# Attention scores from rounded halves: a four-layer transformer kernel on one core

## The reference, cut to what matters

```python
# even, heads 0-7: q, k normed and turned (rope); 8 query heads, 2 key heads; window of 2 chunks and a sink
scores = einsum('bcqhgd,bclhd->bchgql', qc, kb) / sqrt(64)
# even, heads 8-15: q, k normed, own keys per head, relative bias
scores = einsum('bcqhd,bclhd->bhcql', qc, kb) / sqrt(64) + bias
# odd, 8 heads, each with two query and two key parts of 64
s1, s2 = einsum(q1, k1) * scale, einsum(q2, k2) * scale; a = softmax(s1) - lam * softmax(s2)
# MLA, 8 heads: 128 plain dimensions, 64 turned ones whose key is shared by all heads
scores = (einsum(qn, k_nope) + einsum(qr, k_rope)) * scale
```

## Time and profile before

| | us |
|---|---|
| median of 3 runs (2354.4 to 2359.03) | 2355.05 |
| the profiled execution | 2356.17 |
| its span | 2354.4 |
| PE busy | 2172.7 (92%) |
| DVE busy | 1017.2 (43%) |
| ACT busy | 930.6 (40%) |
| POOL busy | 794.7 (34%) |

### The profile page before, as it was taken

How to read it: one execution, slowest core, us unless ns; L and a number is a source line. 1 busy time by engine, 2 the same in 40 slices (tenths; PEclk the granted TensorE clock), 3 DMA queues, 4 the chain that set the end, 5 groups by cost and what they waited for, 6 DMA issues and landing times.

```text
span 2354.4 us, 24410 instructions
## 1 busy us (share of the span) xinstructions
PE 2172.7 (92%) x9534; PEld 1663.5 (71%) x9534; DVE 1017.2 (43%) x1986; ACT 930.6 (40%) x1610; POOL 794.7 (34%) x367
## 2 busy tenths in 40 slices
PE   6999988988987899999979798999979996999997
PEld 5856666855554788888857587888856675888875
DVE  1145443035555246667662644430234446343214
ACT  4234333234444244555441534442244424444323
POOL 3421113432220333333214344444442224444443
PEclk9979999989888899999989899999999998999998
DMA  4210102311100221221112132233311121323331
GB/s 169 91 35 28 36 18 82 106 54 36 36 27 18 79 82 59 68 72 63 63 36 89 46 103 90 90 96 99 95 51 35 51 63 56 98 97 99 96 95 60
DMA packets 47634, 162.99 MB, mean 69 GB/s; under 512 B 5408, under 2 KB 8096, under 8 KB 47392
## 3 DMA queue, kind: packets, MB, share of 16 engines
q1 hardware_dynamic: 47088, 160.06, 21.3%
q10 hardware_dynamic: 432, 1.39, 0.2%
HBM read 159.33 MB, written 2.10 MB: 69 GB/s over the span
## 4 chain that ended last, share of the span: by engine, by line
PE 82%; DVE 10%; ACT 6%; issue 1%; DMA 0%; POOL 0%; ACTq 0%; DVEq 0%
PE ps L1451 22%; PE ps L1454 21%; PE ps L1452 21%; PE ps L1489 4%; PE ps L1505 2%; PE ps L1472 2%; DVE small L1876 1%; PE ps L1582 1%; PE ps L1497 1%; PE ps L1572 1%; PE ps L1466 1%; PE ps L1465 1%; PE ps L1463 1%; PE ps L1477 1%; DVE res L2086 1%
## 5 line engine op out<-in xcount | busy, mean ns | idle before, releaser
L2142 POOL TENSOR_TENSOR wl<-st,wh 128x1024 fp32r<-128x1024 f32 (+2 forms) x312 | 723.6, 2322 | 1372.4 <-ACT wh L1604 1372.3
L1451 PE MATMUL ps<-xh,wh 128*128 128x512 f32 x1520 | 637.0, 419 | 48.4 <-DVE xl L2090 27.9
L1454 PE MATMUL ps<-xh,wl 128*128 128x512 f32 x1520 | 602.5, 396 | 3.0 <-POOL wl L2142 3.0
L1452 PE MATMUL ps<-xl,wh 128*128 128x512 f32 x1520 | 601.6, 396 | 0.0
L1604 ACT ACTIVATE wh<-st 128x1024 fp32r<-128x1024 f32 (+2 forms) x312 | 311.4, 1003 | 240.3 <-PE ps L1454 194.1
L1451 PEld LDWEIGHTS ps<-xh,wh 128*128 128x128 f32 x1520 | 291.3, 192 | 154.5 <-issue 42.2
L1454 PEld LDWEIGHTS ps<-xh,wl 128*128 128x128 f32 x1520 | 290.7, 191 | 67.3 <-POOL wl L2142 3.8
L1452 PEld LDWEIGHTS ps<-xl,wh 128*128 128x128 f32 x1520 | 291.8, 192 | 60.7 <-issue 7.8
L2112 DVE SCALAR_TENSOR_TENSOR tmp<-ps,vec,tmp 128x511 f32<-128x511 f32 (+1 forms) x176 | 131.9, 749 | 258.1 <-ACT tmp L1781 255.0
L1451 PE MATMUL ps<-fa_h,wh 128*128 128x512 f32 x352 | 139.8, 397 | 0.0
L1454 PE MATMUL ps<-fa_h,wl 128*128 128x512 f32 x352 | 139.0, 395 | 0.0
(11 more groups left out here) (246 smaller groups left out, 3022.1 us busy)
## 6 DMA issues: line engine op xcount, KB each, us to landing
st<-in_f_up SPq DMA_DIRECT2D x88, 512.0 KB, 3.5
st<-in_s_xbc SPq DMA_DIRECT2D x32, 512.0 KB, 3.4
st<-in_f_dn SPq DMA_DIRECT2D x32, 512.0 KB, 3.5
st<-in_o_fm SPq DMA_DIRECT2D x24, 512.0 KB, 3.4
st<-in_e_fm SPq DMA_DIRECT2D x22, 512.0 KB, 3.5
st<-in_s_z SPq DMA_DIRECT2D x16, 512.0 KB, 3.5
st<-in_s_out SPq DMA_DIRECT2D x16, 512.0 KB, 3.7
st<-in_f_dn SPq DMA_DIRECT2D x16, 384.0 KB, 3.1
```

The source lines that it names most:

```text
L1451: e.matmul(u.bank.ap, hi, x.h[:, kk, :], start=first, stop=False)
L1452: e.matmul(u.bank.ap, hi, x.l[:, kk, :], start=False, stop=False)
L1454: e.matmul(u.bank.ap, lo, x.h[:, kk, :], start=False, stop=last).then_inc(S["mm"], 1)
L2142: e.tensor_tensor(P.mem["wl"][w.m % NWR][:, 0:w.n], P.mem["stage"][w.m % NSTAGE][:, 0:w.n], P.mem["wh"][w.m % NWR][:, 0:w.n].bitcast(F32), ...
```

## The change

Each query and key is split once into a rounded half and a remainder (`halves`: `head_hi` on ACT, `head_lo` on DVE). Queries of the even and odd layers go into four 128-partition tiles: hi and lo for each of the two heads, where the other head's 64 partitions are zero. The keys stay together, hi and lo. A score is then three one-pass products on 128 partitions. In MLA the plain part has three products; for the turned part one tile holds the hi of the query in one half of the partitions and its lo in the other, so that two products (by the shared key's hi and lo) suffice, five in all. MLA keys get a ring of two in the place of all eight heads. The sliding heads of the even layer are paired anew: unit j holds head j of the first group and head j of the second, so one key unit with both key heads serves all four, and the host reorders the columns of the weights. Tiles move in SBUF: the gates `sg` share the place of `yh`, and MLA's probabilities that of `xh` and `xl`.

```diff
@@ -331,7 +331,26 @@
-    def qk_prep_g(self, u, gcol, dst, rope, done=None):
+    def halves(self, src, ready, dst, parts, freed=()):
+        ends = []
+        his = [self.put("head_hi", src[rows, :], hi, ready, [dst.freed, list(freed)]) for rows, hi, lo in parts]
+        for a, (rows, hi, lo) in zip(his, parts):
+            ends.append(self.put("head_lo", src[rows, :], hi, lo, a))
+        dst.ready = ends
+        return ends
+    def split_q(self, src, ready, dst):
+        h0, h1, l0, l1 = dst.ap
+        up, down = slice(0, 64), slice(64, 128)
+        return self.halves(src, ready, dst, [(up, h0[up, :], l0[up, :]), (down, h1[down, :], l1[down, :])])
+    def split_k(self, src, ready, dst):
+        hi, lo = dst.ap
+        return self.halves(src, ready, dst, [(slice(0, 128), hi, lo)])
+    def qk_prep_g(self, u, gcol, dst, rope, key, done):
@@ -341,16 +360,17 @@
         st.release(ta)
-        g = self.tmp.take() if rope else dst
+        g = self.tmp.take()
         b = self.put("qk_n", g, u, gcol, r, tr)
...
             yield 1
-            self.rope(g, dst)
-        if done:
-            done()
+            x, g = g, self.tmp.take()
+            self.rope(x, g)
+        g.release(*(self.split_q if key == "q" else self.split_k)(g.ap, g.ready, dst))
+        done()
 
@@ -625,6 +645,8 @@
+    for h0, h1, l0, l1 in mem["qz"]:
+        P.zeroed = [P.put("zero", z) for z in (h0[64:128, :], h1[0:64, :], l0[64:128, :], l1[0:64, :])]
@@ -663,8 +685,7 @@
-    kd = [Use(Slot(mem["e_kd"][j])) for j in range(2)]
-    qs, ks = ring(mem["qs"]), ring(mem["ks"])
+    qs, ks = ring(mem["qz"]), ring(mem["kz"])
@@ -674,17 +695,16 @@
-                dst = pool if key == "k" and rope else pool.take()
+                dst = pool.take()
...
-                return P.qk_prep_g(u, P.V(gain), dst, rope, done)
+                return P.qk_prep_g(u, P.V(gain), dst, rope, key, done)
...
-        items = [item(0, 12, "a_kn", kd[0], True, "k"), item(2, 13, "a_kn", kd[1], True, "k")]
-        items[1] = (lambda: True, *items[1][1:])
+        items = [item(0, 12, "a_kn", ks, True, "k")]
...
-            items += [item(fb, 10 + fb, "b_qn", qs, False, "q"), item(fb, 14 + fb, "b_kn", ks, False, "k")]
+            items += [item(fb, 9 + fb, "b_qn", qs, False, "q"), item(fb, 13 + fb, "b_kn", ks, False, "k")]
@@ -711,22 +731,23 @@
-            kb = 2 * (fb // 2) if fb < 4 else fb
+            kb = 0 if fb < 4 else fb
...
+            kh, kl = k.ap
...
-                    h = 2 * fb + hh
-                    ro = slice(64 * hh, 64 * hh + 64)
+                    h = fb + 4 * hh if fb < 4 else 2 * fb + hh
+                    qh, ql = q.ap[hh], q.ap[2 + hh]
...
-                        v, tv = (lambda kb, g=fb // 2: va[:, kb, g * 64:g * 64 + 64]), tva
+                        v, tv = (lambda kb, g=hh: va[:, kb, g * 64:g * 64 + 64]), tva
@@ -735,11 +756,13 @@
-                    tile = Tile([(q.ap[ro, :], k.ap[ro, :])], i, kb0, n, 0.125, mx=mx.ap[:, j:j + 1],
+                    tile = Tile([(qh, kh), (ql, kh), (qh, kl)], i, kb0, n, 0.125, mx=mx.ap[:, j:j + 1],
...
-                    score(P, tile, masks, add, [q.ready, k.ready, tb])
-                    q.release(tile.scored)
-                    k.release(tile.scored)
+                    score(P, tile, masks, add, [q.ready, k.ready, tb, P.zeroed])
+                    if j == 7:
+                        q.release(tile.scored)
+                    if j == 7 and fb > 2:
+                        k.release(tile.scored)
@@ -867,14 +890,15 @@
+            kh, kl = k.ap
...
-                    ro = slice(64 * a, 64 * a + 64)
-                    tile = Tile([(q.ap[ro, :], k.ap[ro, :])], i, 0, n, 0.125, mx=small.ap[:, 4 * a + 1:4 * a + 2],
+                    qh, ql = q.ap[a], q.ap[2 + a]
+                    tile = Tile([(qh, kh), (ql, kh), (qh, kl)], i, 0, n, 0.125, mx=small.ap[:, 4 * a + 1:4 * a + 2],
@@ -882,8 +906,9 @@
-                q.release(tile.scored)
-                k.release(tile.scored)
+                if i == 3:
+                    q.release(tile.scored)
+                    k.release(tile.scored)
@@ -1275,8 +1299,10 @@
-    P.rope(g, kr)
-    qn, qr, rs, pr = (ring(mem[n], over) for n in ("m_qn", "m_qr", "r8", "m_p"))
+    krope = P.tmp.take()
+    P.rope(g, krope)
+    krope.release(*P.split_k(krope.ap, krope.ready, kr))
+    qn, kn, qr, rs, pr = (ring(mem[n], [over, x_read]) for n in ("m_qn", "m_kn", "m_qr", "r8", "m_p"))
@@ -1285,20 +1311,22 @@
-                    tk[h] = P.put("kn_in", kn[:, h, :], u, over)
-                    u.bank.release(tk[h])
+                    tk[h] = kn.take()
+                    u.bank.release(*P.split_k(u.bank.ap, u.done, tk[h]))
...
-                    q = qn.take()
-                    q.ready = [P.put("q_in", q, u)]
-                    u.bank.release(q.ready[0])
-                    got[h] = q
+                    got[h] = qn.take()
+                    u.bank.release(*P.split_k(u.bank.ap, u.done, got[h]))
...
+                    turned = P.tmp.take()
+                    P.rope(g, turned)
...
-                    P.rope(g, r)
+                    up, down = slice(0, 64), slice(64, 128)
+                    turned.release(*P.halves(turned.ap, turned.ready, r, [(up, r.ap[0][up, :], r.ap[0][down, :]),
+                                                                          (down, r.ap[1][down, :], r.ap[1][up, :])]))
@@ -1330,16 +1358,19 @@
-            q, r = got[h], rot[h // 2]
+            q, k, r = got[h], tk[h], rot[h // 2]
...
-            ro = slice(64 * (h % 2), 64 * (h % 2) + 64)
+            (qh, ql), (kh, kl), qrot, (krh, krl) = q.ap, k.ap, r.ap[h % 2], kr.ap
...
-                tile = Tile([(q.ap, kn[:, h, :]), (r.ap[ro, :], kr.ap[ro, :])], i, 0, n, scale,
+                tile = Tile([(qh, kh), (ql, kh), (qh, kl), (qrot, krh), (qrot, krl)], i, 0, n, scale,
...
-                score(P, tile, [], (caus, n - 128, n), [q.ready, r.ready, kr.ready, tk[h]])
-                q.release(tile.scored)
-                r.release(tile.scored)
+                score(P, tile, [], (caus, n - 128, n), [q.ready, r.ready, kr.ready, k.ready])
+                if i == 3:
+                    q.release(tile.scored)
+                    k.release(tile.scored)
+                if i == 3 and h % 2:
+                    r.release(tile.scored)
@@ -1792,11 +1823,11 @@
-        elif kind == "kn_in":
-            dst, u, freed = o
-            act.wait_ge(u.done)
+        elif kind == "head_hi":
+            src, hi, ready, freed = o
+            act.wait_ge(ready)
...
-            e.activation(dst, u.bank.ap, ACT.Copy).then_inc(S["kn_in"], 1)
+            e.activation(hi, src, ACT.Copy).then_inc(S["head_hi"], 1)
@@ -2116,6 +2147,13 @@
+        elif kind == "zero":
+            z, = o
+            e.memset(z.bitcast(F32), 0.0).then_inc(S["zero"], 1)
+        elif kind == "head_lo":
+            src, hi, lo, rounded = o
+            dve.wait_ge(rounded)
+            e.tensor_tensor(lo, src, hi.bitcast(F32), ALU.subtract).then_inc(S["head_lo"], 1)
@@ -2241,18 +2279,17 @@
-        row = lambda name, off, n: [at(f"{name}{i}", off + 2 * K * i, [128, 512]) for i in range(n)]
-        mem["qs"], mem["ks"] = row("qs", q, 2), row("ks", q + 4 * K, 2)
-        mem["pr"] = row("pr", q + 8 * K, 3)
-        q += 14 * K
-        mem["e_sg"] = at("e_sg", q, [128, 8, 512])
-        mem["e_va"] = at("e_va", q + 16 * K, [128, 4, 128])
-        mem["e_vb"] = at("e_vb", q + 18 * K, [128, 4, 512])
-        mem["e_bias"] = at("e_bias", q + 26 * K, [128, 8, 256])
-        mem["e_kd"] = row("e_kd", q + 34 * K, 2)
-        mem["o_sg"] = at("o_sg", q, [128, 8, 512])
-        mem["o_v"] = at("o_v", q + 16 * K, [128, 4, 1024])
-        mem["p2"] = row("p2", q + 32 * K, 2)
+        row = lambda name, off, n, dt=F32: [at(f"{name}{i}", off + 2 * K * i, [128, 512], dt) for i in range(n)]
+        sets = lambda name, off, count, n: [row(f"{name}{j}_", off + 2 * K * n * j, n, F32R) for j in range(count)]
+        mem["qz"], mem["kz"] = sets("qz", q, 2, 4), sets("kz", q + 16 * K, 2, 2)
+        mem["pr"] = row("pr", q + 24 * K, 3)
+        q += 30 * K
+        mem["e_sg"] = mem["o_sg"] = at("sg", R1, [128, 8, 512])
+        mem["e_va"] = at("e_va", q, [128, 4, 128])
+        mem["e_vb"] = at("e_vb", q + 2 * K, [128, 4, 512])
+        mem["e_bias"] = at("e_bias", q + 10 * K, [128, 8, 256])
+        mem["p2"] = row("p2", q, 2)
+        mem["o_v"] = at("o_v", q + 4 * K, [128, 4, 1024])
@@ -2272,11 +2309,11 @@
-        mem["m_kn"] = at("m_kn", q, [128, 8, 512])
+        mem["m_kn"], mem["m_qn"] = sets("m_kn", q, 2, 2), sets("m_qn", q + 8 * K, 2, 2)
...
-        mem["m_kr"] = row("m_kr", q + 32 * K, 1)[0]
-        mem["m_qn"], mem["m_qr"], mem["m_p"] = (row("m_qn", q + 34 * K, 2), row("m_qr", q + 38 * K, 2),
-                                                row("m_p", q + 42 * K, 3))
+        mem["m_kr"] = sets("m_kr", q + 32 * K, 1, 2)[0]
+        mem["m_qr"] = sets("m_qr", q + 36 * K, 2, 2)
```

(18 more changed lines are left out.)

## The result

The change made the kernel slower: 2386.56 us, median of 4 runs (2386.11 to 2386.79), against 2356.93 (2354.4 to 2359.03, 4 runs). The ratio is 1.0126, 95% interval 1.0108 to 1.0143. The forecast was 2315, range 2280 to 2350.

The account below looks back on a forecast made before the run. The prediction took TensorE (82% of the chain) as the bound. Its 81 us saving less 20, 13, 3 and 5 left 40; 2356.2 less 40 and 1.1 gave 2315 us, range 2280 to 2350.

Parts of the forecast that it names:

- term b): Even and odd layers: ACT stands in order before the hi copy, delaying work behind it; 13 us, bounds 0 and 45.
- PE's saving: Attention stages: cheaper score products and the dropped second key unit take 81 us at full clock off PE.
- the five overlapped pairs: First pair and four odd head ends: old 64-row scores overlap; rounded ones take 1.20 us in series, nothing given up.
- rival C: Scores: narrow rounded matmuls cost like fp32; 2335 at 128 columns (10%), 2391 if at 256 too (2%).
- Term a): Even and odd head starts: scores wait for added copy and subtraction, 1.4 us each time; 20 us, bounds 0 and 40.
- Term c): MLA: a bank is freed 0.69 us later, after ACT and DVE; 3 us, bounds 0 and 15.
- Term d): Clock: longer waits can bring stretches at 1.2 GHz, denser scores can take them away; 5 us, bounds -15 and +20.
- The signs that the prediction had named against itself: Odd stage falls by 20 us or grows, or its low-clock time moves by over 20 us from 65.
- Rival D: Slower by chains: ACT blocked behind hi copies, PE waits at each tile, low clock holds; 2365 to 2389, 6%.

Follow-up runs that it names:

- e1: Changed kernel with only the single key unit kept: fp32 score products on 64 rows (MLA 128 and 64), no splitting; 2350.97 us, ratio 0.9970 to the kernel before.
- e2: Changed kernel with its rounded score products, but queries and keys not split, all products reading one rounded tile; 2299.9 us, ratio 0.9761 to the kernel before.
- e9: e2 with the hi copies and lo subtractions of even and odd layers put back, into tiles no score reads; 2339.67 us, ratio 0.9923 to the kernel before.
- e4: Changed kernel with the rounding to hi moved from ACT to DVE; 2410.97 us, ratio 1.0231 to the kernel before.
- e7: Changed kernel with three rounded products on the head's 64 rows in even and odd layers, no zero padding; 2416.89 us, ratio 1.0244 to the kernel before.

## Why the prediction was wrong

The forecast was 40 us faster, and 30 slower was measured. Most of the difference stands in two places: term b), sized at 13 where the runs show 45, and waits that the old, longer scores had covered, which were in no term.

- **PE's saving** was 81, and about 75 came. By the prices above, 32, 48, 24 and 24 tiles of 128 to 512 columns save 57 us in even and odd; the five overlapped pairs (two scores with nothing between them) take back some 7 and the narrow tiles behind a wait some 3: 47, where 50.1 stood. MLA saves 21.5 for 23.7, the key unit 6.3 (e1) for 7.2. Three errors nearly cancel, which was luck: narrow products cost 0.112 and not 0.067 us (rival C at 128 columns in part, between its bounds), a 64-row tile had cost 0.41 and not 0.31, and the pairs did give something up (1.46 us for most before, 1.78 to 1.97 after, where 1.20 was forecast).
- **Lost cover** was in no term, and that is a step that failed. e2 adds no step, and yet PE's waits in the three stages are 22 us longer than in e1, in 22 more waits; each also uncovers the 0.17 us of latency, 4 more. The fall in low-clock time gives some 8 to 11 of that back. The prediction said "unless PE then waits", but it sized such waits only for the added steps.
- **Term a), the chain to the score**, was 20. Its step is right to 0.05 us, and the waits for keys and queries rose by 15.6. As time it is worth 24 (e9 against the change).
- **Term b), the orders of ACT and DVE**, was 13; e9 puts it at 45 in even and odd, with the clock that it costs. This step failed. I counted only ACT standing behind rope, at 10 of the units. DVE stands too, behind ACT (29 us over the span), and its added work comes ahead of masks and maxima; a head without rope pays as well. How the 45 divide between ACT and DVE is open: e4 was to tell, and its collisions with POOL hide it.
- **Term c), MLA**, was 3: the stage lost 12 (151.0 against e2's 138.8) and its start 4, the latter ahead of its first score. How much is the late bank and how much the DVE steps was not separated.
- **Term d), the clock**, was 5. Low-clock time rose by 68 us, at half speed 34 at the most. The balance is -75 of PE, +75 of waits (85 to 160 in even, odd, MLA and its start) and some 6 of latency in 35 more waits; of the +30 this leaves an estimated 24 for the clock. It is part of what a), b) and c) measured, so it does not come on top. Its bound was +20.
- The signs that the prediction had named against itself both came: the odd stage grew (by 17 us), and its low-clock time moved by 24.
- **Rival D** was the outcome, at 6% and 2365 to 2389, and for its reason: chains and low clock. Where it was wrong is the place: PE did not wait at each tile, but at head starts, transposes and norm products, a few times per head.
- The range took each term's bound, but then weighted them as if independent. Waits, lost cover and clock come together.

## What to carry to other kernels

Where one engine is 92% busy by overlapping short chains of two others, taking work off it is worth what remains after the chains: measure the square (old or new work, with or without the helper steps) before the whole. A step added to an in-order engine can cost everything queued behind it, also when its engine is half idle and nobody waits for its result: 45 us for 45 pairs of 0.63 and 0.69 here. And price idle gaps of TensorE twice, as the gap and as the slow stretch behind it; useless matmuls in a known gap gained 0.5% without and 0.9% with the splits. When you price an instruction by the distance of starts, take its neighbours on both sides in: the kind of product shifts where the time is counted.

## What the hardware showed that I had not expected

- A rounded matmul of 128 columns with its own weight load takes 0.112 us; 256 columns cost nearly the same (0.118). The Trainium skill ("TensorE: Matmul & The Clock Gate", LDWEIGHTS) puts a weight load at its columns divided by 1.2 in ns, so an estimate of 107 ns for 128 columns, which would fit as a floor here; no run shows that the load is what sets it. The Trainium skill ("TensorE: Matmul & The Clock Gate", Back-to-back issue gap) gives 81 ns as the sustained distance for 128 columns, which the scores here don't reach.
- A score tile on 64 rows among 128-row work costs 0.39 to 0.41 us more than on 128 rows, as one fp32 product (before) and as three rounded ones (e7). Between fp32 and rounded products on 128 rows nothing is lost, as the forecast said; the first rounded product only has the rest of the fp32 one in its distance.
- A rounding copy of 128x512 took 0.42 us on DVE (e4) for 0.63 on ACT, but 2.5 when it began beside a POOL split, and a subtraction 2.7.
- 16 fillers of 1.8 us made the kernel 22 and 11.5 us faster.
